# A hybrid attention trunk on one core: q and k of the stick-breaking mixer turned by DMA in place of TensorE, its scores and sums two chunks later

## What is computed

```
xn = RMSNorm(x); h = xn @ W_in            # 2956 columns, shared out among four mixers A, B, C, D
# A, stick-breaking attention, 4 heads of 64:
z       = q @ k.T * 64**-0.5              # per head, strictly causal mask
log1m   = where(mask, log_sigmoid(-z), 0)
between = reverse cumsum(log1m) - log1m
a       = where(mask, exp(log_sigmoid(z) + between), 0);  o_A = a @ v
# B: differential attention on q, k after RMS norm and rotary; C: block attention; D: three sparse branches
merged  = sum_i sigmoid(xn @ Wg_i + bg_i) * (o_i @ Wb_i)
x = x + merged @ W_out;  x = x + SwiGLU(RMSNorm(x))
```

## Time and profile before

| what | value |
|---|---|
| median of 3 runs | 836.74 us (836.25 to 837.12) |
| the profiled execution, its own time | 836.82 us |
| its span, first to last instruction | 834.6 us |
| TensorE busy (PE) | 829.7 us, 99% |
| VectorE busy (DVE) | 555.9 us, 67% |
| ScalarE busy (ACT) | 465.8 us, 56% |
| GpSimd busy (POOL) | 263.5 us, 32% |

### The profile page before, as it was taken

How to read it: one execution, slowest core, us unless ns; L and a number is a source line. 1 busy time by engine, 2 the same in 40 slices (tenths; PEclk the granted TensorE clock), 3 DMA queues, 4 the chain that set the end, 5 groups by cost and what they waited for, 6 DMA issues and landing times.

```text
span 834.6 us, 11178 instructions
## 1 busy us (share of the span) xinstructions
PE 829.7 (99%) x4122; PEld 681.1 (82%) x4122; DVE 555.9 (67%) x821; ACT 465.8 (56%) x715; POOL 263.5 (32%) x273
## 2 busy tenths in 40 slices
PE   9999999999999999999999999999999999999998
PEld 6888888878888888888888888887888888888886
DVE  5576888757866666655454688887587666666542
ACT  6886655665455545543457775547544654554441
POOL 0078773004303333320000889530052034233100
PEclk9999999999999999999999999999999999999999
DMA  9745674454548777785565466745535588777752
GB/s 328 270 142 187 204 227 152 152 181 162 201 166 230 218 210 222 219 223 183 168 216 185 151 202 188 222 143 180 189 138 200 188 218 227 223 210 217 218 180 74
DMA packets 100822, 163.06 MB, mean 195 GB/s; under 512 B 37792, under 2 KB 40224, under 8 KB 100512
## 3 DMA queue, kind: packets, MB, share of 16 engines
q1 hardware_dynamic: 100480, 162.07, 62.0%
q10 hardware_dynamic: 288, 0.27, 0.1%
HBM read 153.40 MB, written 1.05 MB: 185 GB/s over the span
## 4 chain that ended last, share of the span: by engine, by line
PE 98%; DMA 1%; issue 0%; SPq 0%; ACT 0%; DVE 0%
PE acc L721 90%; PE att L801 1%; PE att L883 1%; PE att L768 1%; PE att L858 1%; DMA w_raw<-in_w_in 1%; PE att L874 1%; PE att L793 1%; PE acc L801 0%; PE acc L858 0%; PE att L842 0%; PE att L896 0%; PE att L960 0%; PE att L951 0%; PE att L843 0%
## 5 line engine op out<-in xcount | busy, mean ns | idle before, releaser
L1214 DVE TENSOR_TENSOR w_lo<-w_raw,w_hi 128x1024 fp32r<-128x1024 f32 (+1 forms) x276 | 363.7, 1330 | 154.4 <-ACT w_hi L984 151.7
L721 PE MATMUL acc<-w_hi,xt 128*128 128x512 f32 (+1 forms) x1728 | 433.5, 393 | 0.5 <-ACT xt L1007 0.5
L984 ACT ACTIVATE w_hi<-w_raw 128x1024 fp32r<-128x1024 f32 (+1 forms) x275 | 286.7, 1052 | 170.5 <-PE acc L721 164.8
L721 PEld LDWEIGHTS acc<-w_hi,xt 128*128 128x128 f32 x1728 | 318.2, 188 | 65.1 <-ACT w_hi L984 0.9
L721 PE MATMUL acc<-w_lo,xt 128*128 128x512 f32 (+1 forms) x864 | 229.8, 388 | 0.0
L721 PEld LDWEIGHTS acc<-w_lo,xt 128*128 128x128 f32 x864 | 162.0, 188 | 32.9
L1465 POOL TENSOR_SCALAR small<-small 128x2 f32<-128x2 f32 (+4 forms) x14 | 9.3, 664 | 209.9 <-ACT sq_dump L1084 132.4
L1593 POOL TENSOR_TENSOR merged<-merged,prod 128x1024 f32<-128x1024 f32 x10 | 32.4, 3243 | 128.4 <-DVE prod L1263 127.6
L1576 POOL COPY hid_halves<-hid 128x512 uint16<-128x512 uint16 x44 | 45.6, 1064 | 66.7 <-DVE hid L1291 66.7
L1585 POOL COPY hid_t<-hid_halves_t 128x512 uint16<-128x512 uint16 x44 | 35.3, 831 | 95.2 <-DMA hid_halves_t<-hid_halves 80.8
L721 PE MATMUL acc<-w_hi,ht_hi 128*128 128x512 f32 x176 | 47.7, 390 | 0.0
(11 more groups left out here) (179 smaller groups left out, 697.7 us busy)
## 6 DMA issues: line engine op xcount, KB each, us to landing
w_raw<-in_w_ffn SPq DMA_DIRECT2D x88, 512.0 KB, 3.9
w_raw<-in_w_gate SPq DMA_DIRECT2D x64, 512.0 KB, 3.3
w_raw<-in_w_ffn_down SPq DMA_DIRECT2D x44, 512.0 KB, 4.0
w_raw<-in_w_in SPq DMA_DIRECT2D x39, 512.0 KB, 4.8
w_raw<-in_w_branch SPq DMA_DIRECT2D x16, 512.0 KB, 3.3
w_raw<-in_w_out SPq DMA_DIRECT2D x16, 512.0 KB, 3.2
bg<-in_b_gate SPq DMA_DIRECT2D x8, 512.0 KB, 5.4
w_raw<-in_w_in SPq DMA_DIRECT2D x8, 396.0 KB, 3.6
```

What stands on the lines that cost most here:

```text
L721: return pe.matmul(acc[bank0 + t][:, 0:N], x_part[:, k0 + k, t * P:(t + 1) * P], w_part[:, k, 0:N], start=first, stop=last)
L984: act.activation(w_hi[:, n % WR, :, 0:N], w_raw[:, n % RAW, :, 0:N], copy).then_inc(s_hi, 1)
L1214: dve.tensor_tensor(w_lo[:, n % WR, :, 0:N], w_raw[:, n % RAW, :, 0:N], w_hi[:, n % WR, :, 0:N].bitcast(F32), ALU.subtract).then_inc(s_lo, 1)
```

## The change

Mixer A's q and k lose their transposes on TensorE and their copies on ScalarE. GpSimd scales q in place, deals q and k into halves at place 4, SyncE turns them at place 12 of its own order (ahead of the load of chunk 12), and GpSimd joins them at place 9. `z` and `sp` move from places 9 and 14 to 11 and 16, `cum` from 13 and 17 to 15 and 19. `prep B` (13), `Bq` (19), `Bk` (20) and A's product with v (21) stay.

```
-TURN_AT = {33: "C", 40: "D"} | {CHUNKS.index(("ffn", j, 3)) + 9: j for j in range(N_FFN)}
+TURN_AT = {12: "A", 33: "C", 40: "D"} | {CHUNKS.index(("ffn", j, 3)) + 9: j for j in range(N_FFN)}
...
-    ... "ngate": 25, "Aq": 6,
-    "Ak": 7, "Az": (9, 14), "Asp": (9, 14), "Acum": (13, 17), "Apv": (21, 21), "Bq": 19, "Bk": 20,
+    ... "ngate": 25, "Adeal": 4,
+    "Ajoin": 9, "Az": (11, 16), "Asp": (11, 16), "Acum": (15, 19), "Apv": (21, 21), "Bq": 19, "Bk": 20,
...
-                    if mixer in "CD":
+                    if mixer != "B":
                         pe.wait_ge(joined.sem, joined.at(l, ("join", mixer)))
...
                         elif kind == "deal":
-                            if a == "C":
-                                srcs = [(proj[:, :, MBQ:MBQ + 2 * MIX], 0, 2 * MIX)]
+                            if a == "A":
+                                pool.wait_ge(proj_out.sem, proj_out.at(l, ("proj", 0)))
+                                settled(pool.tensor_scalar(proj[:, :, SBQ:SBQ + MIX], proj[:, :, SBQ:SBQ + MIX],
+                                                           HD ** -0.5, None, ALU.mult))
+                            if a != "D":
+                                c0 = SBQ if a == "A" else MBQ
+                                srcs = [(proj[:, :, c0:c0 + 2 * MIX], 0, 2 * MIX)]
...
                         elif kind == "join":
                             pool.wait_ge(s_turn, turned(l, a))
-                            last = {"C": ("z", PAIRS["A"] - 1), "D": ("sm", ("B", PAIRS["B"] - 1))}[a]
-                            pool.wait_ge(att_done.sem, att_done.at(l, last))
+                            last = {"A": ("sm", ("C", PAIRS["C"] - 1)), "C": ("z", PAIRS["A"] - 1),
+                                    "D": ("sm", ("B", PAIRS["B"] - 1))}[a]
+                            if l or a != "A":
+                                pool.wait_ge(att_done.sem, att_done.at(l - (a == "A"), last))
```

More of the change, by code:

```diff
@@ L84 @@
     "stats": 1, "stats_f": 3, "lambda": 14, "x": (0, 0, 1, 2), "f": (-2, -1, 2, 3), "m": (-1, -1, 2, 3),
-    "sig": (49, 53, 57, 57), "o": (22, 44, 44, 58), "subln": 38, "prep": (13, 18, 25), "ngate": 25, "Aq": 6,
-    "Ak": 7, "Az": (9, 14), "Asp": (9, 14), "Acum": (13, 17), "Apv": (21, 21), "Bq": 19, "Bk": 20,
+    "sig": (49, 53, 57, 57), "o": (22, 44, 44, 58), "subln": 38, "prep": (13, 18, 25), "ngate": 25, "Adeal": 4,
+    "Ajoin": 9, "Az": (11, 16), "Asp": (11, 16), "Acum": (15, 19), "Apv": (21, 21), "Bq": 19, "Bk": 20,
     "Bsm": (21, 21, 27, 27), "Bp": (21, 24, 27, 29), "Bpt": (24, 27, 29, 32), "Bpv": (27, 29, 33, 35), "Bo": 36,
@@ L149, in steps @@
         put(4 * g + 4, "proj", g)
-    for name in ("Aq", "Ak", "Bq", "Bk", "Dc"):
+    for name in ("Bq", "Bk", "Dc"):
         put(PLAN[name], "qk", name)
-    for mixer in "CD":
+    for mixer in "ACD":
         for kind in ("deal", "join"):
@@ L533, in turned @@
         def turned(l, what):
-            if what in ("C", "D"):
-                return 16 * NT * (2 * l + "CD".index(what) + 1)
+            if what in ("A", "C", "D"):
+                return 16 * NT * (3 * l + "ACD".index(what) + 1)
             return 16 * NT * (l * len(range(what % 2, N_FFN, 2)) + what // 2 + 1)
@@ L616, in _ @@
                     if u in TURN_AT:
-                        (turn if TURN_AT[u] in ("C", "D") else turn_hid)(l, TURN_AT[u])
+                        (turn if TURN_AT[u] in ("A", "C", "D") else turn_hid)(l, TURN_AT[u])
                     if chunk(l, u) > 2:
@@ L774, in qk @@
                 bank_free(l, step)
[L775 to L779, removed]
+                if name == "Dc":
                     pe.wait_ge(act_misc.sem, act_misc.at(l, ("ngate", None)))
@@ L782, in qk @@
                     pe.wait_ge(pool_done.sem, pool_done.at(l, ("prep", name[0])))
-                c0 = {"Aq": SBQ, "Ak": SBQ + MIX, "Bq": DFQ, "Bk": DFK, "Cq": MBQ, "Ck": MBK,
-                      "Dq": NSQ}.get(name)
+                c0 = {"Bq": DFQ, "Bk": DFK}.get(name)
                 for m in range(2):
                     for t in range(NT):
-                        if name == "Dk":
-                            src = kdup[:, t, 2 * m:2 * m + 2, :]
-                        elif name == "Dc":
+                        if name == "Dc":
                             src = kcdup[:, t, m, :, :]
@@ L1022, in qk_copy @@
                 m = 0 if name[1] == "q" else 2
-                act.activation(qkt[name[0] in "BD"][:, m:m + 2, :].rearrange("p m t -> p (m t)"), att[:, TP, :], copy,
-                               scale=HD ** -0.5 if name == "Aq" else 1.0).then_inc(read_act.now(step), 1)
+                act.activation(qkt[1][:, m:m + 2, :].rearrange("p m t -> p (m t)"), att[:, TP, :], copy
+                               ).then_inc(read_act.now(step), 1)
             def pt_free(l, step):
```

## The result

The changed kernel takes **840.72 us** in the median of four runs (840.12 to 841.89), against 836.52 of before (four runs beside it, 836.25 to 837.12): ratio 1.0051, 95% interval 1.0034 to 1.0068. It is slower, and 0.4 us above the forecast of 840.3. The profiled execution took 840.68 us, its span is 838.9, 4.3 us longer than before.

What follows compares the result with a forecast made beforehand. The prediction took TensorE, busy 829.7 of 834.6 us, as the bound: 836.8 + 2.0 (layer 0) + 1.5 (layer 1) = 840.3 us, with 1.9 us of transposes saved and 5.4 us of stall put in; range 836.3 to 846.0.

Steps and rivals of the forecast that it cites:

- Abs, layer 0: First step of z's scores on ScalarE in layer 0, due at 38.92, late by chunk 13's delay of 1.8 us.
- d: Delay of layer 0's scores and prep B by chunk 13's late load behind the turn: 1.8 us, bounds 0.3 and 5.0.
- prep B begins, layer 0: GpSimd's start of prep B in layer 0: 47.73, plus 1.8 us for the late chunk 13.
- prep B begins, behind before's, layer 1: GpSimd's start of prep B in layer 1, 2.23 us later than its 459.47, set by VectorE behind the scores.
- prep B's length: Prep B on GpSimd: 16.6 us, the middle between bounds of 14.6 and 18.5.
- stall at B's q: TensorE idle at B's q waiting for GpSimd's prep B, 2 to 3 us in each layer; 2.4 in layer 1.
- shift of layer 0: Work behind B's q in layer 0 comes 2.0 us later, with Bq at 66.27 for 65.42.
- shift of layer 1: Work behind B's q in layer 1 comes 1.5 us later, with Bq at 478.44 for 478.13.
- rival 3: TensorE's clock falls in the stall at B's q: 2.65 us lost each time, 845.6 us; chance 0.10.
- a sign that the prediction had named for being wrong: On TensorE, matmuls at 0.44 us each behind the stall at B's q.
- rival 2: SyncE's loads bound: transposes hold the queue 5.6 us, chunk 13 late by 5.0 and 1.8, 845.3 us; chance 0.17.
- Rival 1: Prep B is ready at B's q, no stall: 834.9 us, chance 0.08; near-cancelling middle, 836 to 838, 0.15.

Runs made afterwards that it cites:

- Runs 3: The changed kernel with the second sum ahead of B's q at place 19 (rank 3.9 for 5.5): 836.90 us, ratio 1.0004.
- run 4: The changed kernel without GpSimd's four gain multiplications of mixer B's q and k, so computing something else: 833.98 us, ratio 0.9969.
- run 1: The kernel before with only z, softplus and sums moved to the new places, q and k still transposed by TensorE: 841.37 us, ratio 1.0054.
- run 7: The changed kernel with the load of cw at place 16 of SyncE's order for 12, the turn still at 12: 839.21 us, ratio 1.0029.
- run 6: The changed kernel with 16 useless matmuls of 256 columns ahead of TensorE's wait at B's q: 839.28 us, ratio 1.0030.

## Why the prediction was right

**The mechanism** is the one forecast: transposes saved, TensorE sooner at B's q, scores ahead of proj 2, prep B later, a stall of some 2 us in each layer. Runs 3, 4 and 1 show it from three sides: fill the stall, shorten what is waited for, or make the move without the turn.

**Term by term.**

| term | forecast | measured |
|---|---|---|
| Abs, layer 0 | 38.92 + d | 40.24 |
| d, from chunk 13 | 1.8 | 1.3 |
| prep B begins, layer 0 | 49.53 | 49.00 |
| prep B begins, behind before's, layer 1 | 2.23 | 464.66 - 459.47 - 2.95 = 2.24 |
| prep B's length | 16.6 | 16.48, 16.47 |
| stall at B's q | 3.0, 2.4 | 2.12, 2.17 |
| shift of layer 0 | +2.0 | 71.59 - 68.64 = +2.95 |
| shift of layer 1 | +1.5 | 485.64 - 481.35 - 2.95 = +1.34 |

2.95 is what layer 0 hands on. 68.64 and 481.35 are B's k in TensorE's timeline of the kernel before:

```profile
68.64 0.60 PE L793 MATMUL att<-cst,proj 128*128 128x128 f32 x4
...
481.35 0.60 PE L793 MATMUL att<-cst,proj 128*128 128x128 f32 x4
```

Taking prep B between its bounds was right: the four gain multiplies, now without splits beside them, took 2.84 us for 5.92, and the rotation behind them was the part that met VectorE. "GPSIMD Engine Reference" of the Trainium skill, § 1, has GpSimd share its SBUF interfaces with VectorE's two-input instructions; the trace agrees, in the change from the earlier trace rows to the 2.84 us above.

**What was mis-sized.** Layer 0 without the clock is 65.63 - 65.42 + 1.17 = +1.4, not +2.0, mostly by d. Chunk 13 was issued at 32.33, where 32.2 was forecast, but only because two errors ahead of it cancel: the scale took 1.50 us for 1.0 (above the 1.43 weighed beside it, too), the copies 3.43 for 3.89. It then landed 6.9 us after its issue for 7.5. Against that stands rival 3, which I had as a case of its own with 0.10: the clock fell, in one layer, at 1.6 us where I had 2.65 for each. It isn't a rival but a part of the same stall, and a likely one: all four runs of the changed kernel have a mean clock under full. With it came a sign that the prediction had named for being wrong: the eight high products behind the stall of layer 0 took 3.43 us, 0.43 each.

**Luck in the sum.** The shifts of the trace add up to 4.3 us where 3.5 was forecast: 1.6 of the clock, less 0.6 in layer 0 and 0.2 in layer 1. The forecast's 840.3 comes near 840.7 in part because these errors are opposite. It also started from 836.8, 0.3 above the median that before had beside the change, and had no term for the 0.1 to 0.4 us by which time less span is shorter with the turn.

The bounds of d don't follow from their own figures. With the scale at its lower bound of 0.5 us d is 0, not 0.3; with turn C's issues and a landing of 8.0 us it is 4.8 and 1.6 in the two layers, not 5.0 and 1.8, so that rival 2's sum is some 0.4 us too high. The forecast hangs on neither.

**Rival 1** (prep B is ready) was wrong by the waits, but run 4 shows its time within a microsecond, 834.0 for 834.9. **Rival 2** (the loads) holds for its small share: run 7 sizes it at 1.1 us of stall in layer 0 (2.12 to 1.00), run 1 shows that the rest stands without it. The join cost nothing, as said. The rule that the prediction takes from the Trainium skill ("Advanced Engine Details and Errata", § DMA Advanced Topics), by which transposes are as fast as plain DMAs, came out half true in the changed kernel. The halves of layer 0 landed 3.2 and 3.3 us after their issues, where the loads issued from 18 to 60 us have a median of 4.5 (for twice the bytes), but each transpose held the issuing queue for 1.3 us where a load took 0.37, so the sum by the rows was the better one.

## What to carry to other kernels

Where one engine has no time to spare, read for each step that it waits for how much was to spare before (0.14 us here): work saved ahead of such a step comes back as idle time there, beyond what was to spare. A step moved on the bound engine moves on the helpers too; look there for what now stands behind it. Here the scores' Abs, Exp and Ln on ScalarE, with the softplus on VectorE, came ahead of a copy of 1.2 us and put prep B back by 2.2 us in layer 1, where the transposes had cost 0.96 us. And when a stall can't be removed, put later work ahead of the wait: one rank in a table gave back 3.8 us here.

## What the runs showed of the hardware

- The granted clock of TensorE fell to 0.50 behind idle stretches of 2.12, 2.15, 2.17, 2.39 and 3.54 us (a price of 1.6 us in the three traces where it is read above), and stayed full behind two others of 2.17 and 2.22, each in the same execution as one that fell, and behind all of up to 1.29 us at B's q and z. "TensorE: Matmul & The Clock Gate", § Part 1, of the Trainium skill ties the lower level to idleness; the trace agrees, and run 6, in which idle time was replaced by useless products, shows it by removal.
- A pair of DMA transposes of 256 KB each held SyncE's queue for 2.73 us with nothing issued just ahead, 4.17 us behind one chunk's load, and 7.22 us behind a chunk and 1024 KB. A plain load of 512 KB mostly took 0.37.
- GpSimd's multiplication of 128x512 float32 by a constant took 1.50 us, longer per element than a copy in 16-bit halves of twice as many (1.7 us for 1024).
